# Where the linear attention's query and key projection of the next tile stands in a step

## The reference, cut to what matters

```python
(a_gate, a_x, b_q, b_k, b_v, b_qi, b_ki, b_wi, c_q, c_k, c_v, c_g, c_a) = split_cols(xn @ w_in)
y_a, conv_new, h_new = rglru_mixer(...)     # gated linear recurrence
y_b = attn_fn(q, k, v, qi, ki, wi)          # attention to the 256 best keys of each query
y_c, S_new = gla_mixer(c_q, c_k, c_v, c_g, c_a, S0, ...)   # linear attention with decay
x = x + jnp.concatenate([y_a, y_b, y_c], axis=-1) @ w_out
x = x + jnp.square(jax.nn.relu(rmsnorm(x, norm_mlp) @ w_up)) @ w_down
```

## Time and profile before

| | |
|---|---|
| median of 3 runs | 4069.47 us (4065.07 to 4069.73) |
| span of the profiled execution | 4072.7 us |
| TensorE busy | 3569.3 us, 88% |
| VectorE busy | 2124.8 us, 52% |
| ScalarE busy | 1018.2 us, 25% |
| GpSimd busy | 474.9 us, 12% |
| granted TensorE clock, mean | 0.894 |

### The profile page before, as it was taken

How to read it: one execution, slowest core, us unless ns; L and a number is a source line. 1 busy time by engine, 2 the same in 40 slices (tenths; PEclk the granted TensorE clock), 3 DMA queues, 4 the chain that set the end, 5 groups by cost and what they waited for, 6 DMA issues and landing times.

```text
span 4072.7 us, 52249 instructions
## 1 busy us (share of the span) xinstructions
PE 3569.3 (88%) x17850; PEld 2698.7 (66%) x17850; DVE 2124.8 (52%) x4881; ACT 1018.2 (25%) x2269; POOL 474.9 (12%) x637
## 2 busy tenths in 40 slices
PE   5778778888799999999987787787787999999999
PEld 3545555556447999999855554555464489999997
DVE  1347778877523444434323577887773334343344
ACT  2232333233401111111123233333234011111110
POOL 0100000221301000000001000002122000000000
PEclk9888888775999999999998888876768999999999
DMA  4000000237621111111410000002465201111111
GB/s 137 15 21 14 14 11 9 46 56 140 208 80 52 42 42 42 54 51 42 140 46 22 14 14 14 11 14 60 41 173 183 88 32 57 48 42 42 42 42 55
DMA packets 189759, 229.61 MB, mean 56 GB/s; under 512 B 72723, under 2 KB 150613, under 8 KB 189493
## 3 DMA queue, kind: packets, MB, share of 16 engines
q1 hardware_dynamic: 161796, 165.17, 15.1%
q0 software_dynamic: 20416, 50.27, 3.9%
q10 hardware_dynamic: 7280, 10.83, 0.8%
HBM read 203.22 MB, written 22.98 MB: 56 GB/s over the span
## 4 chain that ended last, share of the span: by engine, by line
PE 74%; DVE 10%; issue 5%; ACT 5%; DVEq 2%; SPq 1%; DMA 1%; POOLq 1%; POOL 1%; ACTq 0%
PE bank L1389 13%; PE bank L1390 13%; PE bank L1391 13%; PE bank L1096 10%; PE bank L1382 6%; PE bank L1092 5%; PE bank L1194 4%; DVE arena L1454 2%; ACT arena L709 2%; PE bank L1178 2%; DVE arena L1721 1%; PE bank L1186 1%; PE bank L1307 1%; PE bank L1140 1%; SPq L464 1%
## 5 line engine op out<-in xcount | busy, mean ns | idle before, releaser
L1861 DVE TENSOR_TENSOR x_rows<-x_rows,bank 128x512 f32<-128x512 f32 (+1 forms) x576 | 396.1, 688 | 632.1 <-PE bank L1391 632.1
L1096 PE MATMUL bank<-arena 128*128 128x512 f32 (+5 forms) x1440 | 526.5, 521 | 3.0 <-ACT arena L737 1.5
L1454 DVE TENSOR_SCALAR_CACHE_REDUCE arena<-arena,vectors 128x384 bf16<-128x384 f32 (+7 forms) x434 | 500.0, 1152 | 47.5 <-POOLq L406 15.3
L709 ACT ACTIVATE arena<-bank 128x512 f32<-128x512 f32 (+11 forms) x848 | 325.1, 440 | 772.3 <-PE bank L1096 334.0
L1389 PE MATMUL bank<-xT_hi,w_up_hi 128*128 128x364 f32 (+1 forms) x1536 | 506.0, 329 | 5.3 <-DVE vectors L1842 5.3
L1391 PE MATMUL bank<-xT_hi,w_up_lo 128*128 128x364 f32 (+1 forms) x1536 | 506.0, 329 | 0.0
L1390 PE MATMUL bank<-xT_lo,w_up_hi 128*128 128x364 f32 (+1 forms) x1536 | 505.9, 329 | 0.0
L1389 PE MATMUL bank<-w_down_hi,hidden_hi 128*128 128x512 f32 x1152 | 449.5, 390 | 7.5 <-issue 7.5
L1390 PE MATMUL bank<-w_down_lo,hidden_hi 128*128 128x512 f32 x1152 | 449.6, 390 | 0.0
L1391 PE MATMUL bank<-w_down_hi,hidden_lo 128*128 128x512 f32 x1152 | 449.6, 390 | 0.0
L1096 PEld LDWEIGHTS bank<-arena 128*128 128x128 f32 (+1 forms) x1440 | 254.5, 194 | 254.8 <-issue 226.4
(11 more groups left out here) (251 smaller groups left out, 4369.4 us busy)
## 6 DMA issues: line engine op xcount, KB each, us to landing
w_up_landing<-in_w_up SPq DMA_DIRECT2D x32, 1024.0 KB, 7.3
w_down_landing<-in_w_down SPq DMA_DIRECT2D x32, 1024.0 KB, 4.9
arena<-in_cache_k SPq DMA_DIRECT2D x160, 128.0 KB, 2.7
arena<-in_cache_v SPq DMA_DIRECT2D x160, 128.0 KB, 2.6
arena<-in_cache_v POOLq DMA_DIRECT2D x96, 128.0 KB, 3.1
arena<-in_cache_k POOLq DMA_DIRECT2D x96, 128.0 KB, 2.9
arena<-in_w_in ACTq DMA_DIRECT2D x4, 2048.0 KB, 16.1
out_projection<-in_w_out SPq DMA_DIRECT2D x16, 512.0 KB, 9.7
```

Source lines behind the costliest of these rows:

```text
L709: return act.activation(dst, src, ACT.Copy, scale=scale)
L1096: ins = mm(b[:R, o:o + w], xnT[:, c, 0:R], w_in[:, c, c0:c0 + w], start=c == 0, stop=c == 7)
L1454: ts(junk, sc, cf[:R].bitcast(F32), None, ALU.is_ge, ALU.add, accum_out=cnt[:R])
L1861: tt(x, x, b[P - R:P, :], ALU.add).then_inc(s_took, 1)
```

## The change

C1 of tile s+1 moves from the start of part 7 to part 8, behind G3 and ahead of yc, on TensorE, on ScalarE and in the plan of banks. The two waits that named G3 of tile 8 now name C1, the last piece to read `W_in`. VectorE's list stays as it is, and so does the projection of tile 0 ahead of the steps.

```diff
@@ plan() @@
                         dve += [(l, s, "su")] if s < NT else [(l, s, f"su{b}") for b in range(SB)]
-                    if N_:
-                        act.append((l, s + 1, "C1"))
                 if h >= 1 and A_ is not None:
...
                 if h == 8:
                     if N_:
-                        act.append((l, s + 1, "G3"))
+                        act += [(l, s + 1, "G3"), (l, s + 1, "C1")]
@@ SyncE @@
-                sp.wait_ge(s_full_a, A_AT[l, NT, "G3"] + 1)
+                sp.wait_ge(s_full_a, A_AT[l, NT, "C1"] + 1)
                 for n in range(4):
                     load_k(n)
@@ GpSimd @@
-                        pool.wait_ge(s_full_a, A_AT[l, NT, "G3"] + 1)
+                        pool.wait_ge(s_full_a, A_AT[l, NT, "C1"] + 1)
                         load_v(0)
@@ ScalarE @@
                                 project(s + 1, 5)
-                        if h == 7 and N_:
-                            project(s + 1, 6)
                         if h >= 1 and A_ is not None:
...
                         if h == 8:
                             if N_:
                                 project(s + 1, 7)
+                                project(s + 1, 6)
@@ TensorE @@
                                 project(s + 1, 5)
-                        if h == 7:
-                            if N_:
-                                project(s + 1, 6)
                         if h >= 1 and A_ is not None:
...
                             if N_:
                                 project(s + 1, 7)
+                                project(s + 1, 6)
```

## The result

The changed kernel takes 4097.06 us (median of 4 runs, 4089.82 to 4101.01), the kernel before beside it 4068.32. The ratio is 1.0067 with a 95% interval of 1.0053 to 1.0081, so the change costs some 29 us, where 20 were forecast as a gain. The profiled execution lies at the low end of its runs, with a span of 4088.2 us, 15.5 more than the one of before, which lay at the high end of its own; so the two profiles show only about half of the difference. The mean granted clock is 0.885 against 0.894.

The account below looks back on a forecast made before the run. TensorE's total work was taken to bound steps 0 to 2, VectorE's gate those from step 3. Gains of 10.9 us in layer 0 and 9.1 in layer 1, together 20.0, took the median from 4069.5 to 4049.5 us; range 4039 to 4068.

Parts of the forecast that it names:

- The mechanism of the gain: Steps with a next tile: C1 moved from ahead of the output cuts VectorE's idle wait, at most 3.67 us a step.
- step 4: Both layers: values 2.4 us sooner, so VectorE gains 2.4; GpSimd's root 0.2 later, its slack of 2.77 down to 0.2.
- Steps 0 and 1: Both layers: same TensorE work, but copies, drain and tanh run beside C1; gain 0.6 us a step, at most 1.06.
- Step 2: Sparse attention present, VectorE waits for GpSimd: gain 0.6 us as in the steps before, 1.2 for both layers.
- Steps 3 and 5: VectorE's idle time at the output: 3.0 us gained in step 3 of either layer; step 5, 3.4 (layer 0), 1.9 (layer 1).
- Steps 6 and 7: Head 7's exp comes late: 0.45 us saved, taken back in three of four; 0.3 kept for step 6 of layer 0.
- The queue: GpSimd's in-order list: next heads' root stands behind yc's store, with 2.1 to 2.8 us of slack before VectorE waits.
- (b): Rival, chance 0.25: gaps of 2 to 5 us put TensorE at 1.2 GHz, losing 16 us of 20; 4066, no change.
- (c): Rival, chance 0.07: yc behind a slow C1 stalls VectorE 5 us or more in steps 4 to 7; 40 lost, 4090.

## Why the prediction was wrong

The step that failed is the pricing of what stands behind the new gap: the prediction took the durations of before, at the full clock, for the output, the values and G3, and put the cost of the idle time itself at nothing. In the runs these matmuls ran at the lower clock, G3 took 8.1 to 9.8 us instead of 7.1, and yc came too late for GpSimd.

The mechanism of the gain was named rightly. Its size agrees in the sum, 16 us faster than before with the gap filled (4051.9 us) where 20 were forecast, but not in the parts, so that agreement is in part luck: in that run layer 0 gained 1.9 us of the 10.9 forecast and layer 1 13.3 of 9.1, and step 4, with 2.4 in the sum, lost 0.4 in one and gained 0.1 in the other.

*Steps 0 and 1* (0.6 us each): right in the mechanism. Without attention no gap arises; the output came 3.4 us earlier and the rest of the step was 2.84 longer, a net of 0.5 in step 0 of layer 0 and 0.7 in layer 1. Step 1 gained 1.9 in both, above the bound of 1.06; some 1.1 of it is the scatter of that stretch, since it also appears with C1 in its old place.

*Step 2* (0.6): wrong by 3.5 to 4.1 us. The loss is in the end of the step, +6.16, where G3 ran at the low clock (9.12 us).

*Step 4, the one worked out in full*: the values came sooner as forecast. Counted from the start of head 7's exp they began 2.5 us earlier (at 442.12 after 440.99, against 440.08 after 436.47). But from there to VectorE's copy of the output it took 5.00 us instead of 2.71, so the wait fell only from 2.60 to 2.41. The sentence that failed next is "G3 starts at 443.7, ends 7.1 us later, C1 3.67 after that". The 7.1 was a duration at full clock, read in a step whose gap was 0.65 us; now it took 8.34. In the changed kernel yc came 6.7 us after the start of the gate's last instruction instead of 0.48, and the slack that the text had put at 0.2 us became a wait of 2.58.

*Steps 3 and 5* (3.0 and 3.4 in layer 0): the output came 2.1 and 1.2 us sooner, and the next heads 2.6 and 0.6 later in all. "Some of this slow stretch will now fall on the output matmuls" was said for step 3, and only for that step, and never for G3.

*Steps 6 and 7*: that TensorE would idle 5 us instead of 2.25 was seen (5.57 and 5.22 in step 7), and its price was taken as zero. The time from heads to output rose by 2.2 us in both steps of layer 0.

*The queue* was read rightly: the slack of 2.1 to 2.8 us and the path by which it is spent. With the clock held the slack sufficed in steps 4 and 5 (C1 in both places); with the slow matmuls it did not. The wait for the root rose by 40.6 us, and taking GpSimd's order away gained 61.

*The rivals.* The outcome is (b) and (c) together, and each was priced alone. (b) put the low clock at 16 us lost and no slowdown, since it let GpSimd be late only in the four late steps, while the ends of the steps grew most in steps 2 to 4, by 2.9 to 6.2 us. (c) had the right path and the right sign, but its 4090 us are near by luck: it had 40 us of waits after steps 4 to 7, where the waits for the root are some 9 us in all. It was given 0.07 on the argument that G3, a dense run, keeps the full rate. It does so only when it starts at that rate: in step 3 it took 9.75 us. (b) is the cause that (c) needed, and they should have been one rival with the chance of (b).

The trace of the kernel before already spoke against that argument, in a row that the prediction did not read. In step 6 of layer 1, behind a gap of 0.91 us ahead of head 6's values:

```profile
2674.41 9.63 PE L1096 MATMUL bank<-arena 128*128 128x512 f32 x16
```

The Trainium skill, "TensorE: Matmul & The Clock Gate", section "Why this matters for your kernels", advises against idle gaps between bursts of matmuls. The gaps that it names are longer than those of steps 2 to 5 here (1.22 to 2.34 us). The runs agree with the advice and go beyond it: 45 us lie between the order with its gap open and the same order with the gap filled, which closed the gaps of steps 2 to 5.

## What to carry to other kernels

Before moving a block of matmuls away from a place, look at what TensorE will do there instead; if it will wait, the block may also be what kept the clock up, and everything behind it must be costed at both levels. Where a wait is shortened, follow the engine's list to the next thing in it: here a root that VectorE needs stood behind a store that it does not need, and putting the small computation ahead of the store gained 17.5 us in the old order, more than the move of C1 gained on top of it. When an order is right but its gap is not, a few matmuls of no use in the gap can pay.

## What the runs showed of the hardware that was not expected

The size of the effect. In step 3 the stretch ahead of the output, with TensorE busy 8.54 of 10 us instead of 9.29, had a granted clock of 0.64 instead of 0.83, and the 17.6 us behind it 0.72 instead of 1.00. The low level outlives its cause: with TensorE busy 97% of the time there, the output, head 7's matmuls, the logits and part of G3 still ran slow. And 96 extra products in all, 8 in each of steps 2 to 7 of both layers, lifted the mean granted clock of the launch from 0.885 to 0.900 and took 45 us off it.

The length of the last gap alone does not tell whether the clock falls. Step 3 of the change, with 1.41 us, has the slow G3, and step 6 of layer 0 with the gap filled, with 2.07 us left, has the fast one:

```profile
637.50 1.33 PE L1191 MATMUL bank<-arena 128*128 128x64 f32 x10 [2.07 <-ACT arena L707]
...
645.19 7.13 PE L1093 MATMUL bank<-arena 128*128 128x512 f32 x16
```

In step 6 of layer 1 of that run 2.43 us were left, and G3 took 9.64. In its step 0 of layer 0 the clock even fell without any idle time, at 118.3 behind the output's narrow matmuls, and G3 took 8.44. What decides between such cases no run here takes apart.
